# Projections that are used as features by tokens, computed with the weights as the stationary operand

## The reference

```python
# first layer
proj = jnp.matmul(u, w_in)      # u: normalised tokens; splits follow
h_a = _mlstm_chunkwise(heads(ml_q), heads(ml_k), heads(ml_v), i_pre, logf)
qkv = _causal_conv_silu(dn_qkv, dn_conv_w)       # 4 taps along the tokens
h_b = _gated_delta_chunkwise(l2norm(q), l2norm(k), v, beta, g)
# second and third layer
h = x @ w_in                    # a_q a_k a_v a_z b_q b_k b_v b_z b_lr m_q m_z
y_a = chunk_band_attention(a_q, a_k, a_v, rel_table)     # 8 heads of 128
o_b = gla_chunk_recurrence(b_q, b_k, b_v, log_g)         # 4 heads, keys of 64
mk, mv = jnp.split(mem @ w_mem_kv, 2, axis=-1)
y_m = memory_attention(m_q, mk, mv)                      # 4 heads of 128
```

## Time and profile before

| | us |
|---|---|
| median of 3 runs | 2369.42 |
| lowest, highest | 2365.99, 2369.48 |
| profiled execution, span from first to last instruction | 2366.4 |
| PE busy in it | 2277.6 |
| DVE busy | 1315.2 |
| ACT busy | 1133.4 |
| PE's weight loads (PEld) busy | 1908.6 |

### The profile page before, as it was taken

The page is one execution under the profiler, slowest core; times in us unless marked ns, Lnnn a source line. Parts: engine busy times, 40 slices in busy tenths (PEclk is TensorE's granted clock), DMA queues, the critical chain, the costliest instruction groups (busy, mean ns, idle before and its releaser), DMA issues.

```text
span 2366.4 us, 32711 instructions
## 1 busy us (share of the span) xinstructions
PE 2277.6 (96%) x11351; PEld 1908.6 (81%) x11351; DVE 1315.2 (56%) x1509; ACT 1133.4 (48%) x1533; POOL 166.1 (7%) x166
## 2 busy tenths in 40 slices
PE   7999999999999999999999998999999799999995
PEld 6878888888788898888888777878788678788884
DVE  4344554554554757657485545546545655566456
ACT  6354554454434727456382534443544444444443
POOL 5000000000000120302112000000000110000002
PEclk9999999999999999999999998999999899999998
DMA  6666556556556535344353545545365265544553
GB/s 224 191 186 191 175 184 190 178 161 221 182 185 204 149 96 155 113 135 133 114 153 90 189 143 171 174 148 166 126 204 185 95 214 164 158 151 143 187 195 107
DMA packets 210532, 386.43 MB, mean 163 GB/s; under 512 B 20664, under 2 KB 37171, under 8 KB 209504
## 3 DMA queue, kind: packets, MB, share of 16 engines
q1 hardware_dynamic: 205664, 365.61, 49.3%
q0 software_dynamic: 4464, 17.04, 2.2%
q10 hardware_dynamic: 272, 2.10, 0.2%
HBM read 380.43 MB, written 4.26 MB: 163 GB/s over the span
## 4 chain that ended last, share of the span: by engine, by line
PE 82%; issue 7%; ACT 5%; DVE 4%; DMA 1%; POOL 0%; DVEq 0%; ACTq 0%; SPq 0%; POOLq 0%
PE stream_psum L513 23%; PE stream_psum L515 22%; PE stream_psum L514 22%; PE heads_psum L491 3%; PE heads_psum L711 2%; PE heads_psum L722 2%; ACT w_high L912 2%; PE heads_psum L721 2%; ACT work L912 1%; PE heads_psum L843 1%; DVE w_low L1287 1%; DVE work L1452 1%; DMA w_raw<-in_w_mem_kv 1%; PE heads_psum L806 1%; PE heads_psum L785 1%
## 5 line engine op out<-in xcount | busy, mean ns | idle before, releaser
L1287 DVE TENSOR_TENSOR w_low<-w_raw,w_high 128x1024 fp32r<-128x1024 f32 (+2 forms) x700 | 847.8, 1228 | 768.3 <-ACT w_high L912 766.3
L912 ACT ACTIVATE w_high<-w_raw 128x1024 fp32r<-128x1024 f32 (+2 forms) x700 | 714.6, 1047 | 474.3 <-PE stream_psum L515 412.5
L513 PE MATMUL stream_psum<-w_high,x_high 128*128 128x512 f32 x2112 | 844.0, 400 | 3.5 <-ACT proj L912 2.5
L515 PE MATMUL stream_psum<-w_high,x_low 128*128 128x512 f32 x2112 | 824.8, 391 | 0.0
L514 PE MATMUL stream_psum<-w_low,x_high 128*128 128x512 f32 x2112 | 824.1, 390 | 0.0
L513 PEld LDWEIGHTS stream_psum<-w_high,x_high 128*128 128x128 f32 x2112 | 398.1, 188 | 86.5 <-issue 5.9
L515 PEld LDWEIGHTS stream_psum<-w_high,x_low 128*128 128x128 f32 x2112 | 397.4, 188 | 84.2
L514 PEld LDWEIGHTS stream_psum<-w_low,x_high 128*128 128x128 f32 x2112 | 398.3, 189 | 79.0 <-issue 1.9
L513 PE MATMUL stream_psum<-w_high,y_high 128*128 128x512 f32 x640 | 252.5, 395 | 10.5 <-DVE w_low L1287 9.6
L515 PE MATMUL stream_psum<-w_high,y_low 128*128 128x512 f32 x640 | 249.9, 390 | 0.0
L514 PE MATMUL stream_psum<-w_low,y_high 128*128 128x512 f32 x640 | 249.6, 390 | 0.0
(11 more groups left out here) (253 smaller groups left out, 1519.5 us busy)
## 6 DMA issues: line engine op xcount, KB each, us to landing
w_raw<-in_w_in SPq DMA_DIRECT2D x528, 512.0 KB, 4.2
w_raw<-in_w_out SPq DMA_DIRECT2D x128, 512.0 KB, 4.5
w_raw<-in_w_mem_kv SPq DMA_DIRECT2D x32, 512.0 KB, 4.9
work<-rows_scratch POOLq DMA_DIRECT2D x8, 512.0 KB, 5.8
proj<-in_mem SPq DMA_DIRECT2D x2, 1024.0 KB, 7.0
residual<-in_x ACTq DMA_DIRECT2D x1, 2048.0 KB, 12.5
mkv_scratch<-proj POOLq DMA_DIRECT2D x4, 512.0 KB, 3.2
work<-mkv_scratch POOLq DMA_DIRECT2D x2, 1024.0 KB, 8.9
```

The costliest lines, as they stand in the source:

```text
L513: pe.matmul(acc, hi[:, k, sl(m)], w, start=first, stop=False)
L515: last = pe.matmul(acc, lo[:, k, sl(m)], w, start=False, stop=final)
L912: return act.activation(dst, src, func, **kw)
L1287: tt(WL[:, c % RING, 0:width], RAW[:, c % RING, 0:width], WH[:, c % RING, 0:width].bitcast(F32), ALU.subtract).then_inc(lo_done, 1)
```

## The change

Blocks whose content is wanted as features by tokens (30 of them) are computed in that form ("turned"): in every k-tile the four groups of 128 weight columns are the stationary operand in turn and all 256 tokens move. That is 12 matmuls of 256 columns in place of 6 of 512, and one weight load before each. The turned blocks are: block 0 and 2 of the memory (the keys of the two layers), block 0 of every mLSTM group, blocks 0, 1, 2 of every delta-net group, and in each of the two layers m_q, the b block with q and k, and a_q, a_k of both halves. The evacuation copies the same two pieces of 512 and scales q on the way. The transposes and the copies behind them go; the delta net's last tap (ACT) and other taps (DVE) read `proj` instead of `heads_psum`. For the gated linear attention q and k are evacuated straight into `work`. The slots of `proj` are now held until the scores are done (mLSTM, attention) or until the last tap is added (delta net).

```diff
@@ PE, stream
+                            for j in range(4 if b in turned else 0):
+                                acc = SP_[:, pair + j // 2, sl(j % 2, S)]
+                                pe.matmul(acc, w[:, sl(j)], hi[:, k, :], start=first and j % 2 == 0, stop=False, skip_group_check=True)
+                                pe.matmul(acc, wl[:, sl(j)], hi[:, k, :], start=False, stop=False, skip_group_check=True)
+                                last = pe.matmul(acc, w[:, sl(j)], lo[:, k, :], start=False, stop=final, skip_group_check=True)
-                            for m in range(M):
+                            for m in range(0 if b in turned else M):
@@ PE, ml
-                for i, n in enumerate("qk"):
-                    for h in range(2):
-                        for m in range(M):
-                            last = tr(H[:, i, h * S + m * P:h * S + (m + 1) * P], PR[:, m, i * S + h * P:i * S + (h + 1) * P])
-                    last.then_inc(*signal(ML_PE, n))
                 yield from gap(3)
-                q, k, w, F = wk(0, 512), wk(0.5, 512), wk(2, 768), wk(10)
-                pe.wait_ge(*done(ML_ACT, "k", g))
+                q, k, w, F = PR[:, 0, 0:512], PR[:, 1, 0:512], wk(2, 768), wk(10)
@@ PE, dn
-                project(1, 0).then_inc(*signal(DN_PE, "k"))
-                yield
-                project(0, 2).then_inc(*signal(DN_PE, "q"))
-                yield from gap(6)
-                pe.wait_ge(*done(DN_V, "conv133", g))
-                project(2, 0).then_inc(*signal(DN_PE, "v"))
-                yield from gap(9)
+                yield from gap(17)
@@ PE, the streams
-            stream(N_MEM, E_MEM, 4, YH, YL, x_prep())
+            stream(N_MEM, E_MEM, 4, YH, YL, x_prep(), turned=(0, 2))
-                stream(N_ML + g * (4 * NCH), E_ML + 4 * g, 4, XH, XL, ml(g - 1))
+                stream(N_ML + g * (4 * NCH), E_ML + 4 * g, 4, XH, XL, ml(g - 1), turned=(0,))
-            stream(N_DN, E_DN, 4, XH, XL, none())
+            stream(N_DN, E_DN, 4, XH, XL, none(), turned=(0, 1, 2))
-                stream(n + L_A0, e + 5, 4, XH, XL, gla(l, q + 1, 2 * (e + 5)), first_need=e + 5)
+                stream(n + L_A0, e + 5, 4, XH, XL, gla(l, q + 1, 2 * (e + 5)), first_need=e + 5, turned=(0, 1))
...
@@ ACT, stream and dn
-                        f(PR[:, m, sl(slots[b], NBLK)], SP_[:, 2 * (b % 2) + m, :], ACT.Copy).then_inc(evac, 1)
+                        dst = wk(m / 2, NBLK) if slots[b] == QK_IN_WORK else PR[:, m, sl(slots[b], NBLK)]
+                        f(dst, SP_[:, 2 * (b % 2) + m, :], ACT.Copy, scale=scales.get((b, m), 1.0)).then_inc(evac, 1)
-                    if p == 0:
-                        wait_alone(act, *done(DN_PE, "qkv"[c], g))
-                        last = f(CV[:, c, h, :], H[:, b0 + h // 2, sl(h % 2, S)], ACT.Copy, scale=CW[:, bass.ds(g * 4 + (3 * 48 + c * 16 + h), 1)])
+                        last = f(CV[:, c, h, :], PR[:, p, c * NBLK + (h % 2) * S:c * NBLK + (h % 2 + 1) * S], ACT.Copy, scale=CW[:, bass.ds(g * 4 + (3 * 48 + c * 16 + h), 1)])
-                       free=[[done(DN_PE, "q", g - 1)], [done(DN_PE, "q", g - 1)], [done(DN_PE, "v", g - 1)], [done(DN_V, "g", g - 1)]])
+                       free=[[done(DN_V, "conv033", g - 1)], [done(DN_V, "conv133", g - 1)], [done(DN_V, "conv233", g - 1)], [done(DN_V, "g", g - 1)]])
@@ ACT, attend
-                act.wait_ge(*done(steps, "q", n))
-                f(wk(0), bank(2, 2), ACT.Copy, scale=float(P) ** -0.5).then_inc(*signal(act_s, "q"))
@@ DVE, dn and attend
-                                src = H[:, b0 + h // 2, sl(h % 2, S)]
+                                src = PR[:, p, c * NBLK + (h % 2) * S:c * NBLK + (h % 2 + 1) * S]
-                dve.wait_ge(*done(steps, "k", n))
-                dve.tensor_copy(wk(1), bank(0, 2)).then_inc(*signal(AT_V[kind], "k"))
```

More of the change, by code:

```diff
@@ L491, in tr, with stream @@
                 return pe.transpose(dst, src, ident[b0:b0 + n, b0:b0 + n])
-            def stream(n, blocks_before, nblk, hi, lo, side, first_need=None, tiles=tuple(range(0, KT, CH)), small=None):
+            def stream(n, blocks_before, nblk, hi, lo, side, first_need=None, tiles=tuple(range(0, KT, CH)), small=None, turned=()):
                 per = len(tiles)
@@ L767, in attend @@
                     ksrc, vsrc = PR[:, :, NBLK:2 * NBLK], PR[:, :, 2 * NBLK:3 * NBLK]
-                for name, src, b0 in (("k", ksrc, 0), ("q", PR, 2)):
-                    for h in range(4):
-                        for m in range(M):
-                            last = tr(H[:, b0 + h // 2, (h % 2) * S + m * P:(h % 2) * S + (m + 1) * P], src[:, m, sl(h)])
-                    last.then_inc(*signal(steps, name))
                 yield from gap(2)
@@ L784, in attend @@
                     for m, a, b in ((0, 0, n0), (1, n0, n0 + S)):
-                        last = pe.matmul(H[:, h, a:b], qT[:, h * S + m * P:h * S + (m + 1) * P], kT[:, h * S:h * S + b - a], start=True, stop=full)
+                        at = (h % 2) * S
+                        last = pe.matmul(H[:, h, a:b], PR[:, h // 2, at + m * P:at + (m + 1) * P], ksrc[:, h // 2, at:at + b - a], start=True, stop=full)
                         if not full:
@@ L815, in gla @@
                 pe.wait_ge(evac, evac_need)
-                for i, name in enumerate("qk"):
-                    for hp in range(2):
-                        for m in range(M):
-                            last = tr(H[:, i, hp * S + m * P:hp * S + (m + 1) * P], PR[:, m, i * S + hp * P:i * S + (hp + 1) * P])
-                    last.then_inc(*signal(GL_PE, name))
                 yield from gap(2)
@@ L880, in _ @@
             pe.wait_ge(consts, N_CONSTS)
-            stream(N_ML, E_ML, 4, XH, XL, gates(), small=done(G_ACT, "mini"))
+            stream(N_ML, E_ML, 4, XH, XL, gates(), small=done(G_ACT, "mini"), turned=(0,))
             with pe.Fori(1, 4) as g:
-                stream(N_ML + g * (4 * NCH), E_ML + 4 * g, 4, XH, XL, ml(g - 1))
+                stream(N_ML + g * (4 * NCH), E_ML + 4 * g, 4, XH, XL, ml(g - 1), turned=(0,))
             stream(N_GA, E_GA, 4, XH, XL, ml(3))
@@ L919, in high, with stream @@
                 f(WH[:, c % RING, 0:width], RAW[:, c % RING, 0:width], ACT.Copy).then_inc(hi_done, 1)
-            def stream(n, nblk, extra, side, slots=(0, 1, 2, 3), free=(), ahead=(CH * NBLK, 0), per=NCH):
+            def stream(n, nblk, extra, side, slots=(0, 1, 2, 3), free=(), ahead=(CH * NBLK, 0), per=NCH, scales={}):
                 for b in range(nblk):
```

87 lines of the change are left out of this document (38 added, 49 removed).

## The result

The changed kernel takes 2386.66 us (median of 4 runs, 2384.75 to 2388.93) against 2369.45 us before (4 runs, 2365.99 to 2369.99). The ratio is 1.0075, with a 95% interval from 1.0063 to 1.0088: 17.2 us slower, where 7.0 us faster was forecast. The span of the profiled run is 2383.1 us, against 2366.4.

What follows compares the result with a forecast made beforehand. PE, busy 96%, was taken as the bound, time being nearly a count of what it issues. -26.4 + 12.4 + 5 + 2 = -7.0 us on a 2366.4 span, the median 3.0 above: 2362.4 us, range 2342 to 2390.

Steps and rivals of the forecast that it cites:

- r: Start-to-start interval of 256-column matmuls in turned blocks, taken as 115.5 ns; 113.3 changes nothing, 116.7 makes the sum zero.
- What comes: the turned blocks: In 30 turned blocks, 2880 matmuls of 512 columns become 5760 of 256, at 115.5 ns each: 12.4 us more.
- rival (3): Turned blocks: 13.4 ns come with every 128-weight load, 120.1 ns a matmul; 2388.9 us, far end 2421; chance 0.18.
- The floor of the load: In bursts of 16 matmuls, loads of 128 weights overlap one another and come every 111.7 ns, just inside 113.
- Transposes: 240 transposes on PE go, in 30 bursts of 8 at 0.88 us, all on its path: 26.4 us less.
- Heads fed slower, +5 us: Heads' small matmuls inside three turned blocks of three delta-net groups are fed 6 ns slower each: 5 us more.
- The cover of the delta net, +2 us: PE gets faster while DVE's convolutions do not, leaving hardly any cover: 0.5 us a group, 2 us more.
- rival (4): DVE becomes the bound where the transposes were; 10.6 us of delta net stay as w_low waits: 2371.0 us, chance 0.10.
- The rule against the change: The skill's rule judges TensorE by summed weight-load time: 2880 added loads of 188 ns, 541 us, 240 taken away.
- rival 5: Turned blocks: loads can't overlap beside 256 columns, so r is 188 ns, +430 us; 2775 us, chance 0.02.

Runs made afterwards that it cites:

- the forms: Changed kernel with 13 blocks without heads each holding one matmul form (columns loaded/moved), span not compared: 60.0 ns for 64/128, 111.4 for 128/128, 119.9 for 128/256.
- the runs with halves: Kernel before, with half of block 0, block 0, blocks 0-1 or 0-2 of each delta-net loop pass in 256-column pairs: 2371.82, 2378.79, 2383.32, 2385.74 us.

## Why the prediction was wrong

The result lies inside the stated range, at its slow end, and on the other side of no change.

**The size of r.** The step that failed is "What comes: the turned blocks", in the choice of r. It took 115.5 ns from small blocks; the trace showed 120.0, and 5760 x (120.0 - 115.5) = 25.9 us, more than the 24.3 between forecast and result, and on the far side of the 116.7 at which the sum is zero. Both signs that the prediction named for its being wrong came: r is outside 114.7 to 116.3, and PE waits where it did not. Two readings led to 115.5. First, the rows were all of loads of 16 or 48 columns, and I took what differed between them (113.1, 115.5, 116.7) for how well PE was fed. It is not that: in the changed kernel and four others the same 48-column block runs at 113.3 behind the same wait of 1.2 us, and the forms show a pair every 60 ns. It is not the columns either, as a block of 16 came at 120.0. What sets it is open, so a row of that kind could not give r. Second, "113.1 is half of 226.7 less 0.2, so the 13.4 ns go with the columns" was the argument against rival (3). It was a coincidence of two extras: 106.7 + 6.7 and half of 213.3 + 13.4. Rival (3)'s near end, the 13.4 ns with every pair that loads 128 columns, gave 120.1 ns, +38.9 and 2388.9 us; measured were 120.0, +38.4 and 2386.7. Its term is right. That its total is right too is luck: it holds 7 us for the heads and the cover that hardly came, and nothing for the jumps. Its reason is half right: at 256 columns moved the whole extra is there with 128 loaded, but it does not come with every pair (128/128 takes 111.4 ns, not 80), and the line through 16 and 48 has no place in the runs.

**The floor of the load** was right: 111.7 ns from the bursts, 111.4 to 111.7 in the forms from 128 to 224 columns moved. That it lies under 113 did not help, as 256 columns don't come down to it.

**Transposes.** -26.4 us was right where it can be read alone: in the last stream with heads the first block, with one attention's 16 transposes before and no turned form in either kernel, went from 33.63 to 31.87 us, 1.76, and 1.76 were priced. For the copies that went nothing was counted, and no wait of PE for them shows in either kernel.

**Heads fed slower, +5 us.** Wrong: 0. All fifteen bursts of 16 in turned blocks of the changed kernel last 1.95 us, like this one:

```profile
865.37 1.95 PE L702 MATMUL heads_psum<-work 128*128 128x128 f32 x16
```

Before, it was 1.94 to 1.99 where nothing had been waited for and 2.05 behind a wait.

**The cover of the delta net, +2 us.** In the loop none of PE's waits is for w_low; that the turned blocks take back what the transposes gave is argued, not shown. In the last group, whose blocks are not turned, it came as rival (4) had it: waits of 0.57 and 0.94 us for w_low, and 2.27 for y_low where it was 0.9, while 2.0 in the first level went. That group was priced at -2.6 and brought -0.6: 2.0 us given back, of a price of 2 for all four.

**What was in no step.** The jump back, 8.2 us at the two jumps, of which 6.5 went when the loop was written out. The page had the instruction queue's row (74 packets), and the prediction counted instructions by their time and not by their room. The trace of before could have raised the question, as its second pass fetches nothing; how near the loop stood to the length at which it does, only the runs with halves tell.

The sum as it came: +38.4 - 26.4 + 8.2 = +20.2, and -3.5 of smaller things of either sign (start, memory and first mLSTM stream -3.6, the rest of the loop -2.5, last group +2.0, half clock in output projection a +1.7, output projection b and small block -1.2), which makes the +16.7 of the spans. The -2.5 of the loop is spread over its three passes and has no cause that the runs show.

**The rule against the change** (rival 5, judging by the loads' own time): PEld's busy time rose by 132 us and the time by 17; loads do overlap.

## What to carry to other kernels

When operands are swapped so that a 512-column matmul becomes two of 256, price the pair of load and matmul in exactly that size: here 120.0 ns against half of 226.7, 1.28 us a block of 192, which no saving of 8 transposes (0.88 us) pays for. A row with other loaded columns is not a neighbour, however well its interval fits half of the larger one, and a short row seen in one kernel may come at another interval in the next. And when a change makes a loop's body longer, look whether its later passes fetched instructions before: from nothing to 8 packets a pass lay 48 pairs, and every jump back of that loop then cost 1.3 to 2.7 us, in the turned kernels often with a stretch at half clock behind it.

## What the runs showed of the hardware that I had not expected

- A pair with 256 columns moved comes every 120.0 ns with 128 columns loaded, in eleven kernels. With 16 or 48 loaded it comes every 113.3 to 120.0 ns, steadily within a row and differently between kernels. With 512 moved fewer loaded columns are no help: 226.9 with 128 loaded, 229.9 with 64, 231.2 with 16.
- TensorE's loop over 804 pairs ran its later passes without fetching, the one over 852 did not.
- A wait of 2 us on TensorE hung on whether VectorE started 0.09 us ahead of GpSimd or 0.26 us behind it.
